# Gate matrix of a product-key expert layer: one-hot rows in 16-bit numbers, the weight in three 8-bit parts, rows made for four tokens at once

## Chip, cores and metric

One Trainium2 chip, one core. The metric is the device time of one execution in microseconds (us); lower is better.

## What is computed

The reference runs two transformer blocks on 256 tokens of width 1024. The change touches one step of the second block, which is done once in each of its two layers: the product-key expert layer (`peer_ffn`).

```python
def peer_ffn(h, w_q, sub_keys, u_tab, v_tab):
    q = (h @ w_q).reshape(B, S, PEER_HEADS, 2, PEER_DQ // 2)
    scores = jnp.einsum('bshpd,hpkd->bshpk', q, sub_keys)
    s1, i1 = lax.top_k(scores[..., 0, :], PEER_TOPK)
    s2, i2 = lax.top_k(scores[..., 1, :], PEER_TOPK)
    # ... the best 16 of the 16x16 pairs: ids = i1 * 128 + i2
    gate = jax.nn.softmax(top_s, axis=-1)
    ...
        u = u_tab[idx]
        act = gelu(jnp.einsum('thkd,td->thk', u, hx))
        return jnp.einsum('thk,thkd->td', g * act, v_tab[idx])
```

There are 128 x 128 experts and 8 heads, and each head chooses 16 experts for each token, so a token has 128 chosen pairs (first key, second key), each with a weight.

## The kernel before

**No gather.** The kernel multiplies with all experts. For each of 128 first keys n it makes the hidden values of 128 experts for 256 tokens (`up(n)` on TensorE, 24 products of 128x256, since each 32-bit product is made of a rounded high part and a low part), takes the gelu into `slots[:, n, :]` (arena), multiplies by the gates, and runs the second product (`down(n)`). Gates of experts that were not chosen are zero.

**The gates.** Those of tokens 128 to 255 go through a table in DRAM that GpSimd scatters into. Those of tokens 0 to 127 are made on chip, and this is what the change is about. For one token, the gate matrix (second key by first key) is a sum over its 128 choices of a one-hot row of the second key, times a one-hot row of the first key, times the weight. With the choices on the partitions this is one TensorE product of 128x128 by 128x128: `second_rows` (one-hot of the second key) is the stationary operand, `first_rows` (one-hot of the first key, times the weight) the moving one. Both are 32-bit numbers, and the trace shows each such product as two matmul records with two weight loads.

**Groups.** Four tokens are a group (`GROUP`), so there are 32 groups (`N_GROUPS`) in each layer. VectorE makes the rows of a group in `gate_rows(j)`: one TENSOR_TENSOR of 128x512 for `second_rows` (L3210) and four TENSOR_SCALAR of 128x128 for `first_rows` (L3214), one for each token because the weight and the key are scalars of the token's column in `keyed`. Both row tensors have two buffers. TensorE runs `gates(j)` (the four products, into a PSUM bank `Y[j % 4]`, "gather" in the trace), then `up(96 + j)`. VectorE then multiplies the known activations by the gates straight from PSUM (`weigh(j)`, L3224), and ScalarE stores the gates of first keys whose activations are not there yet (`late(j)`), which `late_weigh` (L3234) applies later.

**Order of the work.** Every engine's order is written out by hand. TensorE: `up(0)` to `up(95)`, with three transposes near the end that bring the choices and weights of the 128 tokens into `keyed`; then for j = 0 to 31 `gates(j)`, `up(96 + j)`; then the `down` products. VectorE, in the gate stage: `gate_rows(0)`, the low part of a weight tile (`low`, L3089, ring_low, 128x1024), and then for each j `gate_rows(j + 1)`, `weigh(j)`, `late_weigh(j - 1)`, one `low`. A `low` is what TensorE needs for the `up` of its tile, and it is made two tiles ahead. `rows_ready` is counted by VectorE and waited for by `gates(j)`; `gates_filled` is counted by TensorE and waited for by `weigh(j)` and, two groups later, by `gate_rows`; `gates_stored` is counted by ScalarE and waited for by `gates(j + 4)`. The class `Chain` adds a semaphore count to an instruction (`add`) and waits for it on the same engine (`wait`); `chain.wait()` waits for the last one added.

Of the kernel before, what the change touches and what calls it, by code (L numbers as in the profile page):

```python
# [19 lines left out]
BF16 = mybir.dt.bfloat16  # L20
R32 = mybir.dt.float32r
ALU = mybir.AluOpType
# [4 lines left out]
P = 128  # L27
T = 256
# [16 lines left out]
PEER_HEADS, NKEYS, TOPK = 8, 128, 16  # L45
# [22 lines left out]
GROUP = 4  # L68
# [54 lines left out]
     ("cmp_bias", TT * HEADS * N_CMP), ("cmp_valid", TT)])  # L123
CMP_PITCH = 16
BIASES = 3
CMP_COLS = GROUPS * CMP_PITCH
MEM_FIRST = 2
MEM_FILL = {n: (2 * n, 2 * n + 2) if n < 8 else (n + 8, n + 9) for n in range(1, 24)}
# [53 lines left out]
def build(nc, stream, tiles_in, keys_in, ada_in, c_in, xT_in, rows_in, tables_in, final_in, params_in, consts_in, attn_in,  # L182
          masks_in, out):
    ctx = ExitStack()
    with ctx:
# [5 lines left out]
        def S(name):  # L191
            if name not in semaphores:
                semaphores[name] = ctx.enter_context(nc.semaphore(name))
            return semaphores[name]
# [24 lines left out]
        keyed = sb("keyed", [P, 3, T])  # L219
        identity = consts[:, CONSTS["identity"]:CONSTS["identity"] + P]  # L220
        mean_mat = consts[:, CONSTS["mean"]:CONSTS["mean"] + P]
        iota = consts[:, CONSTS["iota"]:CONSTS["iota"] + P]
# [9 lines left out]
        slots = arena[:, :].rearrange("p (i t) -> p i t", t=T)  # L232
# [5 lines left out]
        def carve(at, *shape, memory=arena):  # L238
            n = math.prod(shape)
            view = memory[:, at:at + n]  # L240
            if len(shape) == 2:
                return view.rearrange("p (a b) -> p a b", b=shape[1])
            if len(shape) == 3:
                return view.rearrange("p (a b c) -> p a b c", b=shape[1], c=shape[2])
            assert len(shape) == 1
            return view
# [47 lines left out]
        expert_low = dense.take(4, T)  # L294
        ring_words = ring[:, :, :].rearrange("p s w -> p (s w)")
        rows = Place(gate_rows_at, SLOTS * PIECE, ring_words)
        first_rows = rows.take(2, GROUP, NKEYS)
        second_rows = rows.take(2, GROUP, NKEYS)
        late_act = rows.take(2, P)
        rows.take(P)  # L300
        gates_at = rows.at + P
        weights = rows.take(TT, PEER_HEADS, TOPK)
        offsets = rows.take(PEER_HEADS, TOPK).bitcast(U32)
# [57 lines left out]
        k_mem.append(a.take(2, T))  # L361
        head_bias = a.take(BIASES, P + T)

# [6 lines left out]
        b = Place(ada.at, NKEYS // 2 * T)  # L370
# [23 lines left out]
        Y = [ctx.enter_context(nc.psum_tensor(f"gather{i}", [P, 512], F32)) for i in range(4)]  # L394
# [7 lines left out]
        def mm(out, lhsT, rhs, start, stop):  # L402
            return nc.tensor.matmul(out, lhsT, rhs, start=start, stop=stop, skip_group_check=True)  # L403
# [307 lines left out]
        def bias_of(u):  # L711
            if u["kind"] == "mla":
                return attn_const("future", TT * T)[:, u["tt"] * T:u["tt"] * T + u["w"]]
            return head_bias[:, u["index"] % BIASES, u["tt"] * P:u["tt"] * P + u["w"]]

# [83 lines left out]
        def _(pe):  # L799
# [687 lines left out]
            def peer(l):  # L1487
# [3 lines left out]
                g0 = N_GROUPS * l  # L1491
# [44 lines left out]
                def gates(j, turns=0):  # L1536

                    pe.wait_ge(S("rows_ready"), g0 + j + 1 + 12 * turns)
                    if j >= 4:
                        pe.wait_ge(S("gates_stored"), g0 + j - 3 + 12 * turns)  # L1540
                    for b in range(GROUP):
                        last = mm(Y[j % 4][:, b * NKEYS:(b + 1) * NKEYS], second_rows[:, j % 2, b, :],
                                  first_rows[:, j % 2, b, :], True, True)
                    last.then_inc(S("gates_filled"), 1)

                def down_mm(n, tt, b, high, first=False):
# [776 lines left out]
        def _(dve):  # L2323
            chain = Chain(dve, S("vector_chain"))
            V = nc.vector

            def wide(ap, n):

                return ap.unsqueeze(1).to_broadcast([ap.shape[0], n, ap.shape[1]])
# [786 lines left out]
            def peer(l):  # L3116
# [3 lines left out]
                g0 = N_GROUPS * l  # L3120
# [81 lines left out]
                lows.until(ahead - 1)  # L3202
                dve.wait_ge(S("keyed_ready"), 3 * (l + 1))

                def gate_rows(j):

                    if j >= 2:
                        dve.wait_ge(S("gates_filled"), g0 + j - 1)
                    t = slice(GROUP * j, GROUP * (j + 1))
                    V.tensor_tensor(second_rows[:, j % 2, :, :], wide(iota, GROUP),  # L3210
                                    keyed[:, 1, t].unsqueeze(2).to_broadcast([P, GROUP, NKEYS]), ALU.is_equal)
                    for b in range(GROUP):
                        at = GROUP * j + b
                        last = V.tensor_scalar(first_rows[:, j % 2, b, :], iota, keyed[:, 0, at:at + 1],  # L3214
                                               keyed[:, 2, at:at + 1], ALU.is_equal, ALU.mult)
                    last.then_inc(S("rows_ready"), 1)

                def weigh(j):

# [30 lines left out]
                def down(n, turns=0):  # L3250
# [4 lines left out]
                    if n + 4 < NKEYS:  # L3255
                        hidden_low(n + 4, turns)

                gate_rows(0)
                lows.until(ahead)
                for j in range(N_GROUPS):  # L3260
# [79 lines left out]
        def _(pool):  # L3340
# [62 lines left out]
            for h in range(HEADS):  # L3403
                if h >= BIASES:
                    pool.wait_ge(S("scores_ready"), UNIT_BASE[1] + biased_unit(h - BIASES) + 1)
                slope = -alibi_slopes(HEADS)[h]
                nc.gpsimd.tensor_scalar(head_bias[:, h % BIASES, 0:P], distance[:, 0:P], slope, None, ALU.mult)
                nc.gpsimd.tensor_scalar(head_bias[:, h % BIASES, P:P + T], distance[:, T:2 * T], slope, None, ALU.mult)\
                    .then_inc(S("bias_ready"), 1)
# [239 lines left out]
```

## Time and profile before

| | us |
|---|---|
| median of 3 runs (2925.16 to 2927.48) | 2926.2 |
| the profiled execution, by its own clocking | 2923.19 |
| its span in the trace | 2921.4 |

| engine | busy us | share of the span |
|---|---|---|
| TensorE, matmul | 2895.0 | 99% |
| TensorE, weight load | 2595.1 | 89% |
| VectorE | 2252.5 | 77% |
| ScalarE | 1548.8 | 53% |
| GpSimd | 706.4 | 24% |

The granted clock of TensorE is full in the whole span. TensorE's matmuls overlap one another, so its busy share says that it has work, not how fast it runs: what it costs is the distance from the start of one matmul to the start of the next. The gate stage of the first layer runs from 1543.57 to about 1661.7 us, that of the second from 2445.15 to about 2563.3 us.

### The profile page before, as it was taken

What the parts mean: (1) busy time and instruction counts of PE and PEld (TensorE: products, weight loads), DVE (VectorE), ACT (ScalarE), POOL (GpSimd) and SP (SyncE); (2) the same over time, 40 slices, a digit from 0 to 9 for tenths busy, and PEclk for the clock granted to TensorE, in tenths of its full rate; (3) what the DMA queues carried; (4) which work ended last, traced back from release to release, by engine and by line L of the source; (5) the groups of instructions that cost most, each with busy time, mean ns of one, the idle gap of its engine ahead of it and who ended that gap; (6) DMA issues with size and microseconds to landing.
All of it is one profiled execution on the core that took longest, in us unless ns stands there. A gap on an engine that the chain in (4) does not pass through costs nothing. (4 is left out here: it accounts for less than half of the span.)

```text
span 2921.4 us, 53132 instructions
## 1 busy us (share of the span) xinstructions
PE 2895.0 (99%) x18354; PEld 2595.1 (89%) x18354; DVE 2252.5 (77%) x4303; ACT 1548.8 (53%) x2587; POOL 706.4 (24%) x542
## 2 busy tenths in 40 slices
PE   9999999999999999999999999999999999999998
PEld 8887888888688899899999988888899999988887
DVE  8885888888676789788869866667778887966666
ACT  5546544555654465555554455555655554455444
POOL 0020111101210000027777011110107777311110
PEclk9999999999999999999999999999999999999999
DMA  8773786876256653257776466786357776566775
GB/s 341 285 290 125 256 303 243 324 290 229 84 175 235 210 200 103 95 173 187 188 188 154 162 216 217 235 284 234 132 174 187 188 188 166 150 205 217 217 217 173
DMA packets 201302, 601.61 MB, mean 206 GB/s; under 512 B 53072, under 2 KB 85968, under 8 KB 173904
## 3 DMA queue, kind: packets, MB, share of 16 engines
q1 hardware_dynamic: 142176, 521.19, 52.8%
q0 software_dynamic: 58272, 75.66, 10.9%
q10 hardware_dynamic: 720, 3.00, 0.3%
q8 instruction: 81, 1.33, 0.2%
q14 instruction: 53, 0.43, 0.0%
HBM read 581.81 MB, written 17.96 MB: 205 GB/s over the span
## 5 line engine op out<-in xcount | busy, mean ns | idle before, releaser
L1674 ACT ACTIVATE dense<-ring 128x1024 fp32r<-128x1024 f32 x542 | 573.4, 1058 | 371.8 <-PE gather L403 341.9
L3089 DVE TENSOR_TENSOR ring_low<-ring,dense 128x1024 fp32r<-128x1024 f32 x542 | 660.9, 1220 | 127.1 <-ACT dense L1674 126.1
L403 PE MATMUL turn<-expert_src_high,ring_low 128*128 128x256 f32 x2600 | 725.0, 279 | 0.0
L403 PE MATMUL turn<-expert_src_high,dense 128*128 128x256 f32 x2288 | 645.5, 282 | 0.3
L3426 POOL DMA_INDIRECT gates<-ring x256 | 483.1, 1887 | 664.5 <-DVE ring L3193 409.1
L403 PE MATMUL turn<-expert_src_low,dense 128*128 128x256 f32 x2288 | 636.4, 279 | 0.0
L403 PE MATMUL gather<-dense 128*128 128x512 f32 x2048 | 631.6, 389 | 0.0
L403 PEld LDWEIGHTS turn<-expert_src_high,ring_low 128*128 128x128 f32 x2600 | 488.7, 188 | 0.0
L403 PE MATMUL turn<-rounded 128*128 128x512 f32 x1392 | 480.1, 390 | 0.5 <-DVE rounded L2507 0.5
L403 PEld LDWEIGHTS gather<-dense 128*128 128x128 f32 x2048 | 384.4, 188 | 80.0
L403 PEld LDWEIGHTS turn<-expert_src_high,dense 128*128 128x128 f32 x2288 | 430.3, 188 | 0.7 <-DVE ring_low L3089 0.7
L403 PEld LDWEIGHTS turn<-expert_src_low,dense 128*128 128x128 f32 x2288 | 429.4, 188 | 0.0
L403 PE MATMUL gather<-ring_low,dense 128*128 128x512 f32 x1024 | 398.4, 389 | 0.0
L403 PE MATMUL turn<-rounded,ring_low 128*128 128x256 f32 x1392 | 386.7, 283 | 2.4 <-DVE ring_low L2541 1.2
L2541 DVE TENSOR_TENSOR ring_low<-ring,rounded 128x1024 fp32r<-128x1024 f32 x262 | 325.2, 1247 | 78.2 <-ACT rounded L1674 78.0
L1674 ACT ACTIVATE arena<-turn 128x256 f32<-128x256 f32 (+13 forms) x365 | 154.0, 423 | 344.0 <-PE turn L403 325.3
L1674 ACT ACTIVATE rounded<-ring 128x1024 fp32r<-128x1024 f32 x262 | 274.2, 1053 | 82.7 <-PE gather L403 79.0
L403 PEld LDWEIGHTS turn<-rounded 128*128 128x128 f32 x1392 | 260.8, 188 | 55.0 <-DVE rounded L2507 0.7
L3239 DVE TENSOR_TENSOR dense<-arena,dense 128x256 fp32r<-128x256 f32 x256 | 108.3, 425 | 247.1 <-ACT dense L1674 247.1
L403 PEld LDWEIGHTS turn<-rounded,ring_low 128*128 128x128 f32 x1392 | 260.8, 189 | 5.0 <-issue 1.5
L3416 POOL DMA_DIRECT2D ring<-gates x128 | 91.0, 711 | 664.1 <-DVE arena L3248 634.9
L403 PEld LDWEIGHTS gather<-ring_low,dense 128*128 128x128 f32 x1024 | 192.2, 188 | 39.6
(329 smaller groups left out, 4152.4 us busy)
## 6 DMA issues: line engine op xcount, KB each, us to landing
ring<-tiles_in SPq DMA_DIRECT2D x544, 512.0 KB
ring<-stream SPq DMA_DIRECT2D x204, 1024.0 KB, 5.8
arena<-ada_in POOLq DMA_DIRECT2D x96, 512.0 KB, 5.0
gates<-keyed SPq DMA_DIRECT2D x16, 1024.0 KB, 8.1
ring<-gates POOLq DMA_DIRECT2D x128, 128.0 KB, 3.4
arena<-tables_in POOLq DMA_DIRECT2D x6, 1024.0 KB, 7.6
gates<-ring POOLq DMA_INDIRECT x256
arena<-keys_in SPq DMA_DIRECT2D x2, 1024.0 KB, 7.7
```

Of the source, the lines that this page charges most:

```text
L403: return nc.tensor.matmul(out, lhsT, rhs, start=start, stop=stop, skip_group_check=True)
L1674: return nc.scalar.activation(out, in_, func, **kw)
L2541: V.tensor_tensor(ring_low[:, slot_of(q), cols].bitcast(R32), ring[:, slot_of(q), cols], w_high[:, 2 * (i % 2) + b, :], ALU.subtract).then ...
L3089: V.tensor_tensor(tile_words(t, ring_low).bitcast(R32), tile_words(t), tile_high[:, t % AHEAD, :], ALU.subtract).then_inc(S("tile_low"), 1)
L3239: V.tensor_tensor(expert_low[:, n % 4, :].bitcast(R32), slots[:, n + 12 * turns, :], expert_high[:, n % 4, :], ALU.subtract).then_inc(S("e ...
L3416: pool.dma_start(gate_tiles[:, s, :, :], gates_by_pair[l][n + GATE_SLOTS * turns])\
L3426: pool.indirect_dma_start(gates_flat[l], bass.IndirectOffsetOnAxis(offsets[:, h, c:c + 1], 0), weights[:, 1, h, c:c + 1], None, bounds_che ...
```

## The change

`iota` copied to 16-bit numbers, four times each, becomes `steps`; the two chosen keys become `choice_bits`; the weight is split into three 16-bit numbers of 8 significant bits each, which add up to it (`weight_bits`). This is done once in each layer in `exact_parts()`, ahead of `gate_rows(0)`. In `gate_rows` one comparison makes the second rows of four tokens, one the first rows of four tokens (a single buffer, `first_rows`), and one multiplication makes the three weighted copies `first_parts`. The token is now the innermost index in these tiles, so TensorE reads them at a step of four 16-bit numbers. `gates(j)` has three products for each token, twelve for a group, which add up in PSUM. `gate_rows` gets one more wait, on `rows_ready` of the group before.

```diff
@@ -123,6 +123,7 @@
+PARTS = 3
@@ -294,10 +295,17 @@
         rows = Place(gate_rows_at, SLOTS * PIECE, ring_words)
-        first_rows = rows.take(2, GROUP, NKEYS)
-        second_rows = rows.take(2, GROUP, NKEYS)
+        first_parts = rows.take(2, PARTS * GROUP * NKEYS // 2).bitcast(BF16)\
+            .rearrange("p j (w i b) -> p j w i b", w=PARTS, b=GROUP)
+        second_rows = rows.take(2, GROUP * NKEYS // 2).bitcast(BF16).rearrange("p j (i b) -> p j i b", b=GROUP)
         late_act = rows.take(2, P)
+        steps = carve(rows.at, GROUP * NKEYS // 2, memory=ring_words).bitcast(BF16)\
+            .rearrange("p (i b) -> p i b", b=GROUP)
         rows.take(P)
+        first_rows = keyed[:, 0, 0:GROUP * NKEYS // 2].bitcast(BF16).rearrange("p (i b) -> p i b", b=GROUP)
+        weight_rest = keyed[:, 0, 0:P]
+        weight_bits = keyed[:, 1, 0:PARTS * P // 2].bitcast(BF16).rearrange("p (w t) -> p w t", w=PARTS)
+        choice_bits = slots[:, NKEYS - 2, P:T].bitcast(BF16).rearrange("p (i t) -> p i t", i=2)
@@ -1539,8 +1547,9 @@
                     for b in range(GROUP):
-                        last = mm(Y[j % 4][:, b * NKEYS:(b + 1) * NKEYS], second_rows[:, j % 2, b, :],
-                                  first_rows[:, j % 2, b, :], True, True)
+                        for w in range(PARTS):
+                            last = mm(Y[j % 4][:, b * NKEYS:(b + 1) * NKEYS], second_rows[:, j % 2, :, b],
+                                      first_parts[:, j % 2, w, :, b], w == 0, w == PARTS - 1)
                     last.then_inc(S("gates_filled"), 1)
@@ -3202,18 +3211,39 @@
+                def exact_parts():
+
+                    V.tensor_copy(steps, iota.unsqueeze(2).to_broadcast([P, NKEYS, GROUP]))
+                    for i in range(2):
+                        chain.add(V.tensor_copy(choice_bits[:, i, :], keyed[:, i, 0:P]))
+                    chain.wait()
+                    chain.add(V.tensor_copy(weight_bits[:, 0, :], keyed[:, 2, 0:P]))
+                    chain.wait()
+                    chain.add(V.tensor_tensor(weight_rest, keyed[:, 2, 0:P], weight_bits[:, 0, :], ALU.subtract))
+                    chain.wait()
+                    chain.add(V.tensor_copy(weight_bits[:, 1, :], weight_rest))
+                    chain.wait()
+                    chain.add(V.tensor_tensor(weight_bits[:, 2, :], weight_rest, weight_bits[:, 1, :], ALU.subtract))
+                    chain.wait()
+
                 def gate_rows(j):
                     if j >= 2:
                         dve.wait_ge(S("gates_filled"), g0 + j - 1)
+                    if j >= 1:
+                        dve.wait_ge(S("rows_ready"), g0 + j)
                     t = slice(GROUP * j, GROUP * (j + 1))
-                    V.tensor_tensor(second_rows[:, j % 2, :, :], wide(iota, GROUP),
-                                    keyed[:, 1, t].unsqueeze(2).to_broadcast([P, GROUP, NKEYS]), ALU.is_equal)
-                    for b in range(GROUP):
-                        at = GROUP * j + b
-                        last = V.tensor_scalar(first_rows[:, j % 2, b, :], iota, keyed[:, 0, at:at + 1],
-                                               keyed[:, 2, at:at + 1], ALU.is_equal, ALU.mult)
-                    last.then_inc(S("rows_ready"), 1)
+
+                    def of(i):
+                        return choice_bits[:, i, t].unsqueeze(1).to_broadcast([P, NKEYS, GROUP])
+
+                    chain.add(V.tensor_tensor(first_rows, steps, of(0), ALU.is_equal))
+                    V.tensor_tensor(second_rows[:, j % 2, :, :], steps, of(1), ALU.is_equal)
+                    chain.wait()
+                    V.tensor_tensor(first_parts[:, j % 2, :, :, :],
+                                    first_rows.unsqueeze(1).to_broadcast([P, PARTS, NKEYS, GROUP]),
+                                    weight_bits[:, :, t].unsqueeze(2).to_broadcast([P, PARTS, NKEYS, GROUP]),
+                                    ALU.mult).then_inc(S("rows_ready"), 1)
@@ -3255,6 +3285,7 @@
+                exact_parts()
                 gate_rows(0)
                 lows.until(ahead)
```

## Rows read from the trace of the kernel before

**Rows 1.** The page, busy time of each engine over the span.
```profile
PE 2895.0 (99%) x18354; PEld 2595.1 (89%) x18354; DVE 2252.5 (77%) x4303; ACT 1548.8 (53%) x2587; POOL 706.4 (24%) x542
```
**Rows 2.** Windows: length, busy us and instructions of each engine, clock; gate stages 1, 2.
```profile
core 0: us, PE busy (x) PEld busy (x) DVE busy (x) ACT busy (x) POOL busy (x), PEclk, DMA share, GB/s
1543.57:1661.70 118.13, 118.13 (x1022) 118.13 (x1021) 111.38 (x253) 52.88 (x131) 46.59 (x32) 1.00 0.54 148
2445.17:2563.30 118.13, 118.13 (x1023) 118.13 (x1022) 111.38 (x253) 52.87 (x131) 54.39 (x36) 1.00 0.54 148
```
**Rows 3.** Timeline of TensorE, gate products of both layers: start, us, operation, count.
```profile
1543.57 1.05 PE L403 MATMUL gather<-ring 128*128 128x128 f32 x8
...
1658.46 1.05 PE L403 MATMUL gather<-ring 128*128 128x128 f32 x8
...
2445.15 1.05 PE L403 MATMUL gather<-ring 128*128 128x128 f32 x8
```
**Rows 4.** Timeline of VectorE ahead of the gate stage of layer 1.
```profile
1505.60 1.23 DVE L3089 TENSOR_TENSOR ring_low<-ring,dense 128x1024 fp32r<-128x1024 f32 x1 [1.57 <-ACT dense L1674]
1508.40 1.23 DVE L3089 TENSOR_TENSOR ring_low<-ring,dense 128x1024 fp32r<-128x1024 f32 x1 [1.57 <-ACT dense L1674]
...
1539.20 1.23 DVE L3089 TENSOR_TENSOR ring_low<-ring,dense 128x1024 fp32r<-128x1024 f32 x1 [1.58 <-ACT dense L1674]
1540.34 0.68 DVE L3210 TENSOR_TENSOR ring<-consts,keyed 128x512 f32<-128x512 f32 x1
1540.95 1.11 DVE L3214 TENSOR_SCALAR ring<-consts,keyed 128x128 f32<-128x128 f32 x4
```
**Rows 5.** Timeline of VectorE, one group near the end of the stage.
```profile
1652.39 0.67 DVE L3224 TENSOR_TENSOR arena<-arena,gather 128x500 f32<-128x500 f32 x1
1652.98 0.27 DVE L3234 TENSOR_TENSOR arena<-arena,ring 128x116 f32<-128x116 f32 x1
1653.17 1.22 DVE L3089 TENSOR_TENSOR ring_low<-ring,dense 128x1024 fp32r<-128x1024 f32 x1
1654.30 0.68 DVE L3210 TENSOR_TENSOR ring<-consts,keyed 128x512 f32<-128x512 f32 x1
1654.90 1.11 DVE L3214 TENSOR_SCALAR ring<-consts,keyed 128x128 f32<-128x128 f32 x4
1655.93 0.68 DVE L3224 TENSOR_TENSOR arena<-arena,gather 128x504 f32<-128x504 f32 x1
```
**Rows 6.** Waits inside the gate stage of layer 1: who for whom, us, times, longest.
```profile
DVE arena L3224 <- PE gather L403: 5.9, 21, 1.3
```
**Rows 7.** Groups of TensorE instructions by form: busy us, mean ns.
```profile
L403 PE MATMUL turn<-expert_src_high,ring_low 128*128 128x256 f32 x2600 | 725.0, 279 | 0.0
L403 PE MATMUL gather<-dense 128*128 128x512 f32 x2048 | 631.6, 389 | 0.0
L403 PE MATMUL gather<-ring 128*128 128x128 f32 x512 | 67.4, 275 | 0.0
L403 PE MATMUL gather<-ring,arena 128*128 128x64 f32 x8 | 1.1, 278 | 0.0
L403 PE MATMUL gather<-arena,ring 128*128 128x30 f32 x4 | 0.5, 253 | 0.0
L403 PEld LDWEIGHTS turn<-expert_src_high,ring_low 128*128 128x128 f32 x2600 | 488.7, 188 | 0.0
```
**Rows 8.** Weight loads of transposes (one line's instructions): duration ns min/median/max.
```profile
L820 PEld LDWEIGHTS gather<-consts,arena x126: 138/141/143, 191.4 to 2122.9; 128*128 128x128 f32 x126
```
**Rows 9.** Timeline of TensorE at products with few moving columns.
```profile
516.29 0.53 PE L403 MATMUL gather<-arena,ring 128*128 128x30 f32 x4
...
516.63 0.97 PEld L403 LDWEIGHTS gather<-ring,arena 128*128 128x128 f32 x8
516.66 1.08 PE L403 MATMUL gather<-ring,arena 128*128 128x64 f32 x8
```
**Rows 10.** Groups of VectorE instructions: count, busy us, mean ns, idle before.
```profile
L3089 DVE TENSOR_TENSOR ring_low<-ring,dense 128x1024 fp32r<-128x1024 f32 x542 | 660.9, 1220 | 127.1 <-ACT dense L1674 126.1
L3248 DVE TENSOR_TENSOR arena<-arena,ring 128x256 f32 (+1 forms) x128 | 53.6, 419 | 0.0
L3210 DVE TENSOR_TENSOR ring<-consts,keyed 128x512 f32<-128x512 f32 x64 | 43.8, 684 | 0.0
L2552 DVE CAST rounded<-hidden 128x256 fp32r<-128x256 f32 x88 | 25.9, 295 | 3.0
L2389 DVE TENSOR_SCALAR arena<-arena,keyed 128x512 f32<-128x512 f32 x20 | 10.0, 543 | 0.4
L3138 DVE CAST ring<-ring 128x64 f32<-128x64 uint32 x16 | 4.0, 247 | 0.0
```
**Rows 11.** Timeline of VectorE, instructions that wait for the one before.
```profile
1491.33 0.18 DVE L3187 TENSOR_REDUCE ring<-ring 128x2 f32<-128x32 f32 x1
1491.54 0.17 DVE L3190 RECIPROCAL ring<-ring 128x2 f32<-128x2 f32 x1
```

## The prediction, made before the changed kernel was built or run

> **What bounds the kernel now.** I read the page first: TensorE is busy 99% of the span, VectorE 77% [rows 1]. The change acts only in two stretches, so I looked at the windows over them: in each gate stage of 118.13 us TensorE has no idle time, and VectorE is busy 111.38 us, 94% [rows 2]. So TensorE sets the pace and VectorE is close behind; any theory must price both. ScalarE, at 53 of 118 us, is no candidate. The first gate products of layer 1 start at 1543.57 and the last at 1658.46, 31 groups later: a group takes 3.706 us [rows 3]. Ahead of the stage, where TensorE runs `up` alone, VectorE's low parts step from 1505.60 to 1508.40, held by the tiles, so an `up` takes 2.80 us [rows 4]. The four gate products of a group therefore cost 3.706 - 2.80 = 0.906 us, which is 0.113 us for each of the eight records. VectorE's demand is 111.38 / 32 = 3.48 us a group. It waits for the gate products before `weigh` only 5.9 us in a stage [rows 6]: it catches up with TensorE and then waits a little.
>
> **TensorE, part by part.** Removed: eight records at 0.113, 0.906 us a group. Added: twelve 16-bit products of 128 moving columns, each with its load of 128 stationary columns. No row shows a 16-bit product, so I bound one. *Lower bound, the stream alone:* a record of 512 columns lasts 389 ns, of 256 columns 279 ns [rows 7]; 256 columns are 110 ns, 128 columns 55 ns, and twelve make 0.66 us. *Upper bound, the load alone:* the eight records with only 64 moving columns last 1.08 us in all; taking one record of 0.278 us off and dividing by seven, their starts are 0.115 us apart [rows 7, 9], no less than with 128 columns. There the 32-bit weight load sets the step. If a 16-bit load is no faster, twelve make 12 x 0.115 = 1.38 us. *Value taken:* a load is not always that long. It lasts 188 ns in an ordinary product [rows 7] but 141 ns in a transpose [rows 8], 47 ns less for the same 128 columns. A 16-bit load moves half the bytes, so I put it next to the quick one: 0.111 - 0.047 = 0.064 us a product (0.111 is the step of the eight gate records, (1.05 - 0.275) / 7 [rows 3, 7]). Twelve make 0.77 us. A group saves 0.906 - 0.77 = 0.136 us, and 64 groups 8.7 us. The repeated stationary operand I count as loaded each time: an `up` uses one high part twice in a row and the trace still has one load for each record [rows 1].
>
> A rule speaks against this value. The Trainium skill (TensorE: Matmul & The Clock Gate, section Back-to-back issue gap) says that in a real stream of weight load and matmul pairs with 128 moving columns the spacing is about 81 ns. No run here shows it yet; by it the twelve would take 0.97 us, and the change would cost some 4 us of TensorE time in place of saving 9.
>
> **VectorE, the rows of a group.** Removed: the stretch from the comparison's start at 1654.30 to the next instruction's at 1655.93, 1.63 us (0.60 for L3210, 1.03 for the four L3214) [rows 5]. Added: two comparisons of 512 and one multiplication of 1536 elements in 16 bits. No row has 16-bit operands. Two-tensor rows go by elements: 256 in 419 ns, 512 in 684, 1024 in 1220 [rows 10], 1.04 ns an element. *Upper bound,* the same per element: 684, 684 and 1220 + 512 x 1.047 = 1756 ns. *Lower bound,* by bytes: 512 short numbers are 256 words, 419 ns; 1536 are 768 words, halfway between 684 and 1220, 952 ns. One-tensor rows show that the engine can go at twice the pace: a scalar operation on 512 takes 543 ns against 684 [rows 10], and the four at 128 start 0.26 us apart, (1.11 - 0.34) / 3 [rows 5]. I take the lower bound, because the new tiles have four tokens side by side, so every operand is read in whole runs of words. The starts of following instructions lie about 0.08 us before the end of the last [rows 5], so the three take 0.34 + 0.34 + 0.87 = 1.55 us, 0.08 less than now. The wait between them costs nothing: the first comparison ends while the second runs. The added wait on `rows_ready` is on a multiplication one whole group back, with `weigh` and a low part between; behind it in VectorE's queue stand the rows of the next group, `weigh` and the low part, but it is over when it is reached. VectorE's demand becomes 3.48 - 0.08 = 3.40 us a group, under TensorE's 2.80 + 0.77 = 3.57. The rows are made one group ahead of their use, so they stay hidden.
>
> The Trainium skill (VectorE: DVE Perf Modes, section The perf-mode tier table) gives a two-tensor operation on 16-bit SBUF data two elements a cycle and one on 32-bit data one. The second half agrees with the 1.04 ns above; of the first no run here shows anything yet.
>
> **The start of the stage.** `exact_parts` stands ahead of `gate_rows(0)`, on a path that has little slack: the rows are begun at 1540.34 and end at 1542.06 [rows 4], and TensorE asks for them at 1543.57 [rows 3], 1.5 us later. By start-to-start steps: the copy of 512 (543 ns, the scalar row) 0.46; two casts of 128, between 247 ns for 64 and 295 for 256, say 0.26, less the overlap, so 0.18 and, as it is waited for, 0.29; two waited-for casts of the weight at 0.29; two subtractions of 128, about 0.29 by the 1.04 ns slope under the 419 ns row, 0.32 with the wait. The gap behind a waited-for instruction is 0.03 us: 1491.33 + 0.18 to 1491.54 [rows 11]. The sum is 0.46 + 0.18 + 0.29 + 2 x 0.29 + 2 x 0.32 = 2.15 us. Rows(0) then end at 1540.34 + 2.15 + 0.34 + 0.34 + 0.95 = 1544.12, and TensorE stalls 0.55 us, with the signal 0.6. Behind it in VectorE's queue are the low part for tile 97 and `gate_rows(1)`, both wanted a group later, so they lose nothing. Without the 1.5 us of slack the whole 2.1 us would show. Layer 2 has the same sequence [rows 2, 3]. TensorE stays the bound afterwards, so 2 x 0.6 = 1.2 us remain.
>
> **Sum.** -8.7 + 1.2 = -7.5 us. Against the profiled execution's own 2923.2 (span 2921.4 and 1.8 around it) that is 2915.7; the median of the runs is 3.0 higher, so the forecast is 2926.2 - 7.5 = 2918.7 us. Its own range, with a product between 0.058 and 0.072 us and a stall of 0.3 to 1.5 us, is 2914 to 2925.
>
> **Rivals.** A measurement of this kernel can tell about 0.2%, 5.9 us, from no change.
>
> 1. *The weight load stays at its 32-bit pace (slower).* On TensorE, in `gates(j)`: twelve products at 0.115 are 1.38 us, 0.474 more than now; 64 times and the 1.2 make +31.5, 2957.7 us. It decides from a step of 0.0755 us, where twelve cost what eight cost now. For it: four more loads a group, in a stage in which loads and streams are equally long. Against: the quick load [rows 8]. The step of 0.081 of the rule above lies between, and so does the 0.092 of the four records with 30 columns, (0.53 - 0.253) / 3 [rows 7, 9]: at the mean of 0.064 and 0.115, 0.09, the group costs 1.08 us, 2938.5 us; at 0.08, 0.96 us, 2930.9 us.
> 2. *VectorE at one element a clock (slower).* The rows take 0.60 + 0.60 + 1.68 = 2.88 us, the demand is 3.48 + 1.25 = 4.73 us against 3.70, VectorE becomes the bound and TensorE waits for `rows_ready`: 32 x 1.02 = 33 us a layer, less about 2.6 us of rows made ahead, 2 x 30 = +60, 2986 us. For it: no two-tensor row is faster. Against: the halved bytes.
> 3. *Streams alone count (faster).* If products that share a stationary operand are not held by its reload, TensorE needs 2.80 + 0.66 = 3.46 us, VectorE 3.40, about even; 64 x 0.246 - 1.2 is -14.5, and some of it is lost to VectorE's late, long groups: 2914 us at most.
>
> **How the numbers follow.** Forecast 0.42, rival 3 0.10, a step between 0.075 and 0.10 0.18, rival 1 in full 0.14, rival 2 0.16. The range reaches from the streams alone, 2911.5, to the full load, 2958, and leaves out rival 2. Faster by over 0.2%: most of the forecast's case and rival 3, 0.45. Within 0.2%: the forecast's slow edge and the low end of the steps between, 0.14. Slower: 0.41.
>
> **What would show it.** Starts of gate groups 3.57 us apart in place of 3.706; twelve records with starts 0.064 apart; comparisons at 420 ns and the multiplication at 950; VectorE still waiting for gates before `weigh`; one TensorE gap near 0.6 us ahead of the first group of each layer. If the comparisons last 680 ns, the prediction fails by rival 2; if the twelve take over 0.9 us, by rival 1.

## The result and the profile after

The changed kernel is slower: 2958.14 us (median of four runs, 2957.95 to 2961.07) against 2926.84 us (2925.16 to 2928.52) for the kernel before, measured beside it. The ratio on record is 1.0115, with a 95% interval of 1.0103 to 1.0126 (the two medians alone give 1.0107). The prediction was 2918.7 us with a range up to 2958.0, so the measured time lies 0.14 us outside the range, on the side opposite to the forecast. It is within half a us of the time worked out for rival 1, 2957.7 us; the runs below show that the mechanism of this rival was another one.

The page of the changed kernel, busy time of each engine (beside [rows 1]):

```profile
span 2956.3 us, 53590 instructions
PE 2929.4 (99%) x18610; PEld 2625.1 (89%) x18610; DVE 2250.0 (76%) x4189; ACT 1549.2 (52%) x2587; POOL 715.0 (24%) x542
```

TensorE is still the engine that always has work, VectorE even has slightly less. The span is 34.9 us longer than that of the kernel before (2956.3 against 2921.4). The windows over the first gate stage from its second to its last group, 30 groups (beside [rows 2]):

```profile
core 0: us, PE busy (x) PEld busy (x) DVE busy (x) ACT busy (x) POOL busy (x), PEclk, DMA share, GB/s
1548.37:1675.47 127.10, 127.10 (x1082) 125.28 (x1081) 103.45 (x182) 48.65 (x120) 44.80 (x28) 1.00 0.47 128
```

The clock is full, TensorE has no idle time, VectorE is busy 81% of the stretch where it was 94%. The time is inside TensorE's own queue. Timeline of TensorE, start and us (beside [rows 3]):

```profile
1544.15 1.57 PE L411 MATMUL gather<-ring 128*128 128x128 bf16 x12 [0.28 <-DVE ring L3243]
1545.48 0.36 PE L411 MATMUL turn<-expert_src_high,dense 128*128 128x256 f32 x1
...
1548.37 1.58 PE L411 MATMUL gather<-ring 128*128 128x128 bf16 x12
1549.71 0.36 PE L411 MATMUL turn<-expert_src_high,dense 128*128 128x256 f32 x1
...
1675.47 1.59 PE L411 MATMUL gather<-ring 128*128 128x128 bf16 x12
```

From 1544.15 to 1675.47 are 31 groups, so a group takes 4.236 us where it took 3.706. The twelve gate products hold the queue from 1548.37 to 1549.71, 1.34 us, 0.112 us for each. The difference, 0.530 us, times 64 groups is 33.9 us, and a stall at the start of each stage brings it to the 34.9 us of the span. The same reading of the kernel before:

```profile
1562.09 1.05 PE L403 MATMUL gather<-ring 128*128 128x128 f32 x8
1562.90 0.37 PE L403 MATMUL turn<-expert_src_high,dense 128*128 128x256 f32 x1
1563.10 0.28 PE L403 MATMUL turn<-expert_src_low,dense 128*128 128x256 f32 x1
1563.22 0.28 PE L403 MATMUL turn<-expert_src_high,ring_low 128*128 128x256 f32 x1
```

Its eight records hold the queue for 0.81 us, and the `up` behind them takes the other 2.90 us of the group, before and after alike: its second product starts 0.20 us behind its first, where the next ones follow 0.12 us apart. So the gate products went from 0.81 to 1.34 us, and the `up` did not move. What kind of time the gate products' is, the groups by form tell (busy us, mean ns; stretch of the first stage; beside [rows 7]):

```profile
L411 PE MATMUL gather<-ring 128*128 128x128 bf16 x377 | 49.9, 297 | 0.3 <-DVE ring L3243 0.3
L411 PEld LDWEIGHTS gather<-ring 128*128 128x128 bf16 x378 | 40.2, 118 | 2.3 <-DVE ring L3243 0.5
```

Here lies the surprise. The weight load is short, 118 ns against 188: the 16-bit load is quicker, as the forecast had it. But the matmul record lasts 297 ns. By [rows 7] a record of 256 columns at one a clock lasts 279 ns and one of 512 lasts 389, so 128 columns should make 224. These 128 columns take as long to stream as some 300 would. One thing about them is new: TensorE reads them at a step of four numbers.

### The profile page after: what moved, and what is told of

The parts are those of the page before. It is cut to its first block and busy times, and to the rows that moved or that the text cites. A ratio compares the mean times of both kernels' runs of the same rounds, so it can differ in the third digit from the quotient of the medians.

```text
span 2956.3 us, 53590 instructions
## 1 busy us (share of the span) xinstructions
PE 2929.4 (99%) x18610; PEld 2625.1 (89%) x18610; DVE 2250.0 (76%) x4189; ACT 1549.2 (52%) x2587; POOL 715.0 (24%) x542
## 5 line engine op out<-in xcount | busy, mean ns | idle before, releaser
L3457 POOL DMA_INDIRECT gates<-ring x256 | 491.5, 1920 | 660.6 <-DVE ring L3202 409.3
```

Source lines behind the costliest of these rows:

```text
L3457: pool.indirect_dma_start(gates_flat[l], bass.IndirectOffsetOnAxis(offsets[:, h, c:c + 1], 0), weights[:, 1, h, c:c + 1], None, bounds_che ...
```

## The experiments

Three theories could give 0.112 us a product. *Stream*: the moving operand at a step of four streams at half pace. *Step of the load*: the loaded operand at a step of four loads slowly. *Load as such*: 128 columns take 0.11 us to load whatever their size. In the runs that read other numbers than they should, VectorE's work, every instruction and every size stay as they are, so only TensorE's addresses differ.

### Which operand it is

The edits, in `gates(j)`:

```diff
 # e1: moving operand adjacent; e2: loaded operand adjacent; e3: both
-    mm(Y..., second_rows[:, j % 2, :, b], first_parts[:, j % 2, w, :, b], ...)
+    # e2, e3: second_rows[:, j % 2, :, :].rearrange("p i b -> p (i b)")[:, b * NKEYS:(b + 1) * NKEYS]
+    # e1, e3: first_parts[:, j % 2, w, :, :].rearrange("p i b -> p (i b)")[:, b * NKEYS:(b + 1) * NKEYS]
```

> The changed kernel, but TensorE reads each moving operand of a gate product from 128 adjacent 16-bit numbers in place of every fourth one; the numbers are then the wrong ones, so the gates of tokens 0 to 127 are not computed rightly, while every instruction and its size stay. The loaded operand keeps its step of four. Theory 'stream' (the moving operand read at a step of four streams at half pace; a gate record lasts 297 ns where 168 + 53 = 221 was to be expected): records fall to about 220 ns, twelve products from 1.34 to about 0.77 us, the group from 4.24 to about 3.6 us, the kernel by 64 x 0.6 = 38 us to about 2920. Theory 'step of the load' and theory 'load as such' (a 128-column load takes 0.11 us each time): no change, 2958.

> The changed kernel, but the loaded (stationary) operand of a gate product is read from 128 adjacent 16-bit numbers in place of every fourth; the gates of tokens 0 to 127 are not computed rightly, every instruction and its size stay. The moving operand keeps its step of four. Theory 'step of the load': twelve products fall from 1.34 to about 0.77 us, the kernel to about 2920. Theory 'stream' and theory 'load as such': no change, 2958 within 3 us.

> The changed kernel with both operands of the gate products read from 128 adjacent 16-bit numbers; the gates of tokens 0 to 127 are not computed rightly, every instruction and its size stay. Theory 'load as such': still 0.11 us for a product, 2958. Theory 'stream': the same as with the moving operand alone packed, about 2920. If both steps matter and each alone hides the other, only this one falls to about 2920 and the two before it stay at 2958.

Moving operand adjacent: 2917.8 us. Loaded operand adjacent: 2956.0 us. Both: 2916.5 us (nine runs, 2914.95 to 2919.51; ratio to the kernel before 0.9973, 0.9963 to 0.9983). The first two are single runs. With the moving operand adjacent, groups of TensorE's gate products by form, and the timeline; then the groups with the loaded one adjacent, and the load with both adjacent:

```profile
L411 PE MATMUL gather<-ring 128*128 128x128 bf16 x372 | 26.7, 221 | 0.3 <-DVE ring L3244 0.3
L411 PEld LDWEIGHTS gather<-ring 128*128 128x128 bf16 x372 | 21.9, 115 | 1.8 <-DVE ring L3244 0.5
```

```profile
1547.02 0.86 PE L411 MATMUL gather<-ring 128*128 128x128 bf16 x12 [0.29 <-DVE ring L3244]
1547.69 0.36 PE L411 MATMUL turn<-expert_src_high,dense 128*128 128x256 f32 x1
...
1657.39 0.86 PE L411 MATMUL gather<-ring 128*128 128x128 bf16 x12
```

```profile
L411 PE MATMUL gather<-ring 128*128 128x128 bf16 x324 | 41.9, 293 | 0.3 <-DVE ring L3244 0.3
L411 PEld LDWEIGHTS gather<-ring 128*128 128x128 bf16 x324 | 34.1, 113 | 1.6 <-DVE ring L3244 0.5
```

```profile
L411 PEld LDWEIGHTS gather<-ring 128*128 128x128 bf16 x303 | 17.0, 98 | 1.1
```

With the moving operand adjacent its record falls to 221 ns, twelve products to 1547.69 - 1547.02 = 0.67 us, the group to (1657.39 - 1547.02) / 31 = 3.560 us. With the loaded one adjacent little changes. The theory 'stream' holds; the other two fall. The load's step of four costs little. Packing it alone takes the group from 4.236 to 4.200 us (starts from 1544.23 to 1674.43 in e2), 2.3 us in 64 groups, which is the difference between the two kernels. Packing it on top of the other shortens its record from 115 to 98 ns, but the group takes 3.566 us (1543.94 to 1654.49 in e3) against 3.560, so nothing is gained. The 1.3 us between the kernel times of e1 and e3 arise ahead of the first gate stage, as told below the table of steps.

### What each product costs

The changed kernel without the third product of each token; the lowest part of the weight is made but left out of the sum.

```diff
-                        for w in range(PARTS):
+                        for w in range(2):
                             ...
-                                      first_parts[:, j % 2, w, :, b], w == 0, w == PARTS - 1)
+                                      first_parts[:, j % 2, w, :, b], w == 0, w == 2 - 1)
```

> The changed kernel without the third of the three products for each token (the lowest part of the weight is made but left out of the sum): 8 products for a group in place of 12. By every theory in which a product costs its own 0.1115 us (1.34 / 12), a group falls by 0.446 us to 3.79 and the kernel by 28.5 us to 2929.5, some 3 us above the kernel before, where eight records of 32-bit numbers cost 0.81 to 0.91 us. If a fixed cost of changing between 16-bit and 32-bit products were most of it, the gain would be well below 28 us.

Measured: 2929.24 us (ratio 1.0016, 1.0006 to 1.0026). Four products of 64 groups less are 28.9 us less, 0.113 us each; in the traces the group falls from 4.236 to 3.766 us ((1660.49 - 1543.74) / 31), 0.118 us each. So the time is the products' own, and no fixed cost of changing between 16-bit and 32-bit products is most of it. It also says that at this pace even two parts would have gained nothing.

### How the pace depends on the step

The moving operand at other steps, from the same tile:

```diff
+    flat = first_parts[:, j % 2, :, :, :].rearrange("p w i b -> p (w i b)")
+    # step s = 3, 8 (step 2 likewise within one part): flat[:, at:at + s * (NKEYS - 1) + 1:s]
```

> The changed kernel, but the moving operand of each gate product is every second 16-bit number in place of every fourth (from the same tile, so the gates of tokens 0 to 127 are not computed rightly); all else stays. Before this, adjacent numbers gave 0.056 us a product and a step of four 0.1115. Theory 'only adjacent numbers stream at full pace': still 0.11 us, 2958. Theory 'distance in bytes' (four bytes are what a 32-bit operand steps by, and those stream at full pace): 0.056 us a product, the group 3.57 us, 2917. Something between, 0.08, would mean a cost that grows with the distance, 2935.

> The changed kernel, but the moving operand of each gate product is every third 16-bit number (6 bytes apart) in place of every fourth; the gates of tokens 0 to 127 are not computed rightly, all else stays. Step 1 and step 2 gave 0.056 and 0.059 us a product, step 4 gave 0.1115. If the pace falls in one step at a distance of 8 bytes, this gives 0.06 us and about 2920; if the cost grows evenly with the distance from step 2 on, 0.085 us and about 2938; if everything over 4 bytes is at half pace, 0.11 us and 2957.

> The changed kernel with the moving operand of each gate product at every eighth 16-bit number (16 bytes apart); the gates of tokens 0 to 127 are not computed rightly, all else stays. If the pace is full up to some distance and half beyond it, as at step 4: 0.11 us a product and 2957. If the cost grows with the distance: 0.2 us or more a product, 12 x 0.1 x 64 = 77 us more, 3030 or more.

Timeline of TensorE, the twelve gate products and the first `up` behind them, at step 2, 3 and 8, one fence for each:

```profile
1563.23 0.90 PE L411 MATMUL gather<-ring 128*128 128x128 bf16 x12
1563.94 0.37 PE L411 MATMUL turn<-expert_src_high,dense 128*128 128x256 f32 x1
```

```profile
1555.73 1.26 PE L411 MATMUL gather<-ring 128*128 128x128 bf16 x12
1556.77 0.37 PE L411 MATMUL turn<-expert_src_high,dense 128*128 128x256 f32 x1
```

```profile
1559.33 2.94 PE L411 MATMUL gather<-ring 128*128 128x128 bf16 x12
1561.90 0.48 PE L411 MATMUL turn<-expert_src_high,dense 128*128 128x256 f32 x1
```

| step of the moving operand, 16-bit numbers | bytes spanned by 128 columns | twelve products, us | one, us | group, us | kernel, us |
|---|---|---|---|---|---|
| 1 (e1, one run) | 256 | 0.67 | 0.056 | 3.560 | 2917.8 |
| 2 (e5, one run) | 512 | 0.71 | 0.059 | 3.605 | 2922.5 |
| 3 (e6, one run) | 768 | 1.04 | 0.087 | 3.95 | 2943.0 |
| 4 (changed kernel) | 1024 | 1.34 | 0.112 | 4.236 | 2958.1 |
| 8 (e7, one run) | 2048 | 2.57 | 0.214 | 6.03 | 3077.8 |

The times of the gate products and of the group (mean over the first stage) are safer here than those of the kernel. In the traces of e1, e5, e6, e7 and e9, and in that of f1 below, the granted clock was 0.50 for 10 to 14 us in all, in two or three stretches near 276, 520 and 800 us, and the first gate stage began at 1547.0 to 1548.8 us; in the other traces that was 0 to 3.4 us, and the stage began at 1543.2 to 1544.4. These 3 to 5 us lie ahead of anything that the runs change.

From step 2 on a product costs 0.027 to 0.030 us for each unit of the step. In bytes, the stream goes over the row at 2048 / 0.214 = 9.6 bytes a ns at a step of eight, 9.1 at four, 8.8 at three and 8.7 at two, gaps included. Adjacent numbers take 56 ns, near one column a clock, 128 / 2.4 = 53 ns at the full clock of 2.4 GHz. Of the expectations for e5, 'distance in bytes' came nearest (0.059 us a product against 0.056), of those for e6 the even growth came true (2943.0 against 2938), and so did that of e7.

The time of e7 holds one thing more. 64 x (2.57 - 1.34) = 79 us would make 3037. The clock is most of the rest. Windows and timeline of e7:

```profile
1550.00:1640.00 90.00, 90.00 (x535) 71.74 (x534) 50.63 (x90) 23.43 (x59) 41.30 (x28) 0.91 0.39 89
1563.00:1566.00 3.00, 3.00 (x16) 3.00 (x16) 2.68 (x5) 0.24 (x1) 2.39 (x3) 0.50 0.17 0
```

```profile
1562.46 0.28 PE L411 MATMUL turn<-expert_src_high,dense 128*128 128x256 f32 x1
...
1563.10 0.41 PE L411 MATMUL turn<-expert_src_low,dense 128*128 128x256 f32 x1
1563.31 0.41 PE L411 MATMUL turn<-expert_src_high,ring_low 128*128 128x256 f32 x1
...
1566.22 0.28 PE L411 MATMUL turn<-expert_src_low,dense 128*128 128x256 f32 x1
```

The granted clock is 0.91 on average, and 0.50, the 1.2 GHz level, behind the twelve slow streams that began at 1559.33: there the `up` products step by 0.21 us in place of 0.12, and that `up` takes 4.56 us. Over the two stages the clock is at 0.50 for some 65 us in all, which at half pace costs about 32 us. Another 0.1 us a group, 6 us, is the last slow stream reaching into the `up`, which takes 3.00 us at the least behind it in place of 2.90, and 4 us lie ahead of the stage. With the 79 that is 121 us, where the kernel grew by 120. In the changed kernel, with streams half as slow, the clock in the stages stayed at 1.00, and so it did in e9 below, where eight streams as slow as these run in each group.

### Is it a matter of 16 bits?

The kernel before, with its 32-bit moving operand at a step of two and of four:

```diff
-                                  first_rows[:, j % 2, b, :], True, True)
+    flat = first_rows[:, j % 2, :, :].rearrange("p b i -> p (b i)")
+    # e8: flat[:, b // 2 * 2 * NKEYS + b % 2:][every 2nd]; e9: flat[:, b:b + 4 * NKEYS - 3:4]
```

> The kernel before (32-bit rows, four products for a group, two records each), but the moving operand is every second 32-bit number, so 8 bytes apart; the gates of tokens 0 to 127 are not computed rightly, all else stays. If it is the distance in bytes that counts, 8 bytes are at half pace here too: each record goes from 107 to 213 ns of stream, a group from 0.9 to some 1.75 us, the kernel by 54 us to about 2978. If the half pace belongs to 16-bit numbers that are not side by side, nothing changes, 2925.

> The kernel before (32-bit rows, four products for a group), but the moving operand is every fourth 32-bit number, 16 bytes apart; the gates of tokens 0 to 127 are not computed rightly, all else stays. The rule that fits the runs so far: a stream of 128 columns takes the longer of its own cycles and of the bytes it spans at 9.6 bytes a ns (step 4 of 16-bit numbers: 1024 bytes, 0.107 us; step 8: 2048 bytes, 0.213). A 32-bit record of 128 columns lasts 107 ns of stream anyway, so 8 bytes apart cost nothing. With 16 bytes apart it spans 2048 bytes: 0.213 us for each of eight records, the group 0.85 us longer, the kernel by 54 us to about 2979. If 32-bit streams are not slowed by distance at all: 2924.

Measured, one run each: 2923.6 us at step 2, beside 2924.95 for the kernel before, and 2986.3 us at step 4, beside 2923.15. The expectation for e8 gave two outcomes and the second came true. That does not mean what it said there, that words are exempt: e9 shows them slowed. The groups by form of e8 and of e9:

```profile
L403 PE MATMUL gather<-ring 128*128 128x128 f32 x193 | 26.0, 275 | 0.0
```

```profile
L403 PE MATMUL gather<-ring 128*128 128x128 f32 x153 | 38.0, 403 | 0.0
```

32-bit gate records start 0.111 us apart at a step of one already, and in that time about 1024 bytes can be passed over, which is just a step of two; e8's groups take 3.713 us against 3.706. Whether those 0.111 us are the stream itself or the 32-bit load is not told apart: the record lasts as long as an `up` record of 256 columns, 275 and 279 ns, but one of 64 columns lasts 278 too [rows 7]. At a step of four it spans 2048 bytes, and the record lasts 403 ns, close to the 409 of a 16-bit one that spans as much. It grows by 128 ns where the rule at 9.6 bytes a ns says 107; the kernel grew by 63 us where 54 were expected, of which 4 to 5 lie ahead of the stage. So the rule holds within some 20% for words too: what counts is the distance in bytes, not the format, and a step that costs nothing behind a slower 32-bit product can take twice the time of a quick 16-bit one.

### Full kernels that avoid the step

Two kernels have all of the computation. In *f4* the first rows are made for two tokens side by side, so TensorE reads at a step of two (4 bytes); the order of the parts is changed so that VectorE's three instructions stay three. In *f1* the weight's parts go into the second rows, which are loaded, and the plain one-hot first rows are made token by token and streamed.

```diff
 # f4
+    first_parts: "p j (h w i b) -> p j h w i b", h=2, w=PARTS, b=2
+    last = mm(Y..., second_rows[:, j % 2, :, b], first_parts[:, j % 2, b // 2, w, :, b % 2], ...)
 # f1
+    V.tensor_tensor(first_rows[:, j % 2, :, :], wide(iota, GROUP), choice_bits[:, 0, t].unsqueeze(2)..., ALU.is_equal)
+    last = mm(Y..., second_parts[:, j % 2, w, :, b], first_rows[:, j % 2, b, :], ...)
```

> A full kernel, all of it computed: the changed kernel with the first rows made for two tokens side by side in place of four, so that TensorE reads the moving operand at a step of two; the rows of the four tokens still come from one comparison and one multiplication, whose token operands are now read two adjacent numbers at a time. Theory 'distance in bytes' for TensorE: 0.67 us for the twelve products, group 3.57, 2917 to 2920. Theory 'only adjacent numbers': 2958. For VectorE: if runs of two 16-bit numbers are read as fast as runs of four, comparison 0.42 and multiplication 0.95 us; if not, up to 0.68 and 1.75, with which VectorE needs some 4.3 us a group and the kernel takes 2960 or more.

> A full kernel, all of it computed: the weight's three parts go into the second rows, which TensorE loads (step of four, which cost nothing so far), and the plain one-hot first rows are the moving operand, made with each token's 128 numbers adjacent. TensorE then needs 0.67 us for twelve, 3.47 to 3.57 us a group. But the comparison of the first rows reads one number of a token again and again, and VectorE does it at one element a clock, 0.68 us in place of 0.42: its demand rises from 3.40 to 3.66 us a group and becomes the bound. Expected 2926 within 4 us, no gain or loss against the kernel before. If VectorE did it in 0.42 us, 2917.

f4: 2919.97 us, ratio 0.9984 (0.9975 to 0.9994). VectorE's comparison took 0.42 us and its multiplication 0.95, so a run of two numbers is read as fast as one of four. Its group takes 3.605 us, as in e5. f1: 2923.02 us, ratio 0.9995 (0.9985 to 1.0005), no difference. VectorE's groups and the window in f1, and the two places where TensorE idled around the end of the first stage:

```profile
L3242 DVE TENSOR_TENSOR ring<-keyed 128x1536 bf16<-128x1536 bf16 x27 | 25.7, 952 | 0.0
L3239 DVE TENSOR_TENSOR ring<-consts,arena 128x512 bf16<-128x512 f32 x27 | 18.5, 685 | 0.0
L3237 DVE TENSOR_TENSOR keyed<-ring,arena 128x512 bf16<-128x512 bf16 x27 | 11.3, 419 | 0.0
```

```profile
1550.00:1640.00 90.00, 90.00 (x910) 88.91 (x910) 90.00 (x151) 40.68 (x100) 76.08 (x26) 1.00 0.60 147
```

```profile
1654.80 0.86 PE L411 MATMUL gather<-ring 128*128 128x128 bf16 x12 [0.32 <-DVE ring L3242]
...
1663.12 0.47 PE L411 MATMUL gather<-dense 128*128 128x512 f32 x1 [0.89 <-DVE dense L3268]
```

Its first-row comparison takes 685 ns, in which one operand is 32-bit and the other repeats one number; which of the two costs it the pace was not told apart. VectorE is busy 90.00 of 90.00 us, so it has no slack left. But it is not yet what sets TensorE's pace in this window: TensorE has no idle time either, and its 910 records are as many as in the same window of e3. VectorE's backlog shows only at the end, as 0.32 and 0.89 us of idle TensorE. The time came out as expected (2926 within 4); that VectorE is the bound throughout did not.

The last one, *f5*, is f4 with a 16-bit format of 11 significant bits, so that two parts carry 22 bits of the weight in place of 24, and a token needs two products.

```diff
-BF16 = mybir.dt.bfloat16
-PARTS = 3
+BF16 = mybir.dt.float16
+PARTS = 2
+        rows.take(GROUP * NKEYS)      # keeps what lies behind the rows in its place
```

> All of the computation is there: as f4_pairs, but with two parts of 11 significant bits (16-bit floating point with a longer fraction) in place of three of 8, so two products for a token and a multiplication of 1024 elements in place of 1536. If a step of two streams at full pace and this format goes like the other: TensorE 8 x 0.056 = 0.45 us, group 2.90 + 0.45 = 3.35, VectorE's demand 3.40 - 0.27 = 3.13; 64 x 0.36 - 1 = 22 us gained on the kernel before, 2903. If the step of two streams at half pace: 8 x 0.11 = 0.89, 2928.

Measured: 2903.06 us (four runs, 2901.08 to 2904.56), ratio 0.9927 (0.9911 to 0.9944), 20.6 us faster than the kernel before. Timeline of TensorE and the groups of f5:

```profile
1543.21 0.66 PE L413 MATMUL gather<-ring 128*128 128x128 f16 x8
...
1647.55 0.66 PE L413 MATMUL gather<-ring 128*128 128x128 f16 x8
```

```profile
L413 PE MATMUL gather<-ring 128*128 128x128 f16 x224 | 18.6, 224 | 0.0
L3250 DVE TENSOR_TENSOR ring<-keyed 128x1024 f16<-128x1024 f16 x29 | 19.8, 684 | 0.0
```

A group takes (1647.55 - 1543.21) / 31 = 3.366 us. It is the fastest kernel of this study.

## Why the prediction was wrong, point by point

**What bounds the kernel.** Right. TensorE sets the pace before and after, with no idle time in the stage.

**TensorE: the value taken, 0.064 us a product.** This is the step that failed. It measured 0.112 us, twelve made 1.34 us in place of 0.77, and 64 times the 0.57 us between them is 36 us. The reasoning on the load was right: it took 118 ns, even shorter than the 141 taken as its neighbour. What was missing is the other operand. The lower bound priced the stream by its columns, from rows of operands whose numbers are adjacent, and nowhere was a price put on the step of four that the change introduces, though the diff shows it. With only this removed (e1) the kernel took 2917.8 us; the sum had said 2918.7. That these two agree is in part luck, since two terms of the sum miss in opposite directions and cancel there: adjacent products cost 0.056 us in place of 0.064, 0.1 us less for twelve, and the next term was 0.1 us too large.

**What is removed: 0.906 us.** This term was mis-sized too. It was the group less an `up` of 2.80 us, taken from a stretch in which `up` runs alone [rows 4]. Behind gate products an `up` takes 2.90 us, in the kernel before and in the changed one, and the eight records held the queue for 0.81 us. The sum took away 0.1 us a group more than was there, 6 us in all. On the profiled executions the forecast was 2915.7 us and the measured time 2958.13, 42 us apart: 36 from the products and 6 from this term. (The medians are only 39 us apart because the forecast put the median 3 us above the profiled execution, and in the changed kernel the two are the same.)

**The rule against this value.** The Trainium skill's spacing of about 81 ns (TensorE: Matmul & The Clock Gate, section Back-to-back issue gap) did not show either: adjacent numbers gave 56 ns, a step of four 112. The Trainium skill (TensorE: Matmul & The Clock Gate, section Weight-path perf modes) says that 16-bit weights of 128 columns load in a fast mode, packed or strided. The load records agree so far that at either step they are well under the 188 ns of 32 bits: 98 ns where both operands are adjacent, 113 to 118 in the other runs. On steps, the Trainium skill (SBUF — State Buffer, the note on cachelines) says that two hits in each line of 16 bytes are needed for full bandwidth, and puts the stride that is free at up to eight 16-bit or four 32-bit numbers. For a moving operand it is not so here: a step of four 16-bit numbers, two hits a line, is at half pace, one of three at two thirds, one of eight at a quarter, and a 32-bit record at a step of four lasted 403 ns in place of 275.

**Rival 1.** Its time came out, 2957.7 us against 2958.1, and its mechanism was wrong. It held the load to its 32-bit pace; e1 and the load records show a quick load. That the time agrees so closely is luck: it put the twelve at 1.38 us and what they replace at 0.906, 0.474 more a group, where 1.34 and 0.81 were measured, 0.53 more, and the 3 us between median and profiled execution filled what was missing. The chance of 0.14 was given to the load alone; the cause that led to this time had none.

**VectorE, the rows.** Right. Timeline of VectorE in the changed kernel, start of the first stage (beside [rows 4, 5]):

```profile
1540.49 0.42 DVE L3216 CAST ring<-consts 128x512 bf16<-128x512 f32 x1
1540.82 0.36 DVE L3218 CAST arena<-keyed 128x128 bf16<-128x128 f32 x2
1541.22 0.31 DVE L3220 CAST keyed<-keyed 128x128 bf16<-128x128 f32 x1
...
1542.47 0.42 DVE L3240 TENSOR_TENSOR keyed<-ring,arena 128x512 bf16<-128x512 bf16 x1
1542.81 0.42 DVE L3241 TENSOR_TENSOR ring<-ring,arena 128x512 bf16<-128x512 bf16 x1
1543.15 0.95 DVE L3243 TENSOR_TENSOR ring<-keyed 128x1536 bf16<-128x1536 bf16 x1
1544.02 1.21 DVE L3098 TENSOR_TENSOR ring_low<-ring,dense 128x1024 fp32r<-128x1024 f32 x1
```

0.42, 0.42 and 0.95 us, from start to start 0.34 + 0.34 + 0.87 = 1.55, each as worked out. Rival 2 had no part in it. The Trainium skill's two elements a cycle for a two-tensor operation on 16-bit data (VectorE: DVE Perf Modes, section The perf-mode tier table) agrees: 512 elements took 0.42 us and 1536 took 0.95, 0.52 ns for each element more, half of the 1.04 ns of 32-bit numbers. VectorE's demand was 103.45 / 30 = 3.45 us a group, where 3.40 had been said.

**The start of the stage.** Right. `exact_parts` took 1542.47 - 1540.49 = 1.98 us for 2.15, and the first gate products began at 1544.15. Before, they began at 1543.57; the stage is 0.15 us later in this run (1540.49 against 1540.34), so 0.43 us are left for the stall, where 0.55 to 0.6 was said; the row shows 0.28 us of idle matmul before it.

**Rival 3.** Half right. A product with adjacent numbers costs 0.056 us, the stream alone, where the forecast's case had 0.064. Twelve made 0.67, within 0.01 of the bound. The gain of e3 was still only 8 us in place of 14, and the 0.1 us a group by which the `up` behind them is longer than 2.80 accounts for 6 of these. VectorE was busy nearly all the time in e1, as the rival had it, but no row shows TensorE held by it inside the stage, and in the changed kernel, where VectorE is busy only 81%, the `up` takes the same 2.90 us. Window of e1:

```profile
1550.59:1657.39 106.80, 106.80 (x1083) 105.54 (x1081) 104.09 (x183) 48.63 (x120) 50.54 (x28) 1.00 0.53 152
```

**The range.** It ended at the full load, 2958, and was missed by 0.14 us. A bound made of one mechanism's exact price, with the whole of that case meant to lie inside, left no room for the spread of the runs (2957.95 to 2961.07).

## What to carry to other kernels

When a layout is changed to suit one engine, price how the other one reads it: here the token was made innermost so that VectorE reads whole runs, and TensorE's moving operand paid for it. Put the operand that must be read at a step on the loading side (f1, which gained nothing here because its rows cost VectorE more), or keep the step of the moving side within four bytes (pairs of 16-bit numbers), which served both engines. When a bound of an unmeasured operation is taken from rows, check that these rows read their operands the way the new operation will. And take the cost of a block that is removed from its own rows (here from its first start to the start of what follows it, 0.81 us) rather than as a difference to another stretch of the kernel (0.906).

## What the runs showed of the hardware

- A moving operand of 128 columns streams at the slower of one column a clock (53 ns at the full clock) and about 9 bytes of span a ns: 0.056, 0.059, 0.087, 0.112 and 0.214 us a product at steps of 1, 2, 3, 4 and 8 16-bit numbers (8.7 to 9.6 bytes a ns). Other numbers of columns were not run.
- A loaded 16-bit operand of 128 columns costs little more at a step of four than adjacent: 0.036 us in a group of twelve beside a moving operand at a step of four, nothing beside an adjacent one. Its record lasts 113 to 118 ns, 98 where both operands are adjacent, and a 32-bit one 188.
- The matmul record shows the step: it lasts 221 ns with adjacent numbers, 297 at a step of four and 409 at eight. Whoever goes by its length alone would read it as one of more columns.
- The stages with very slow streams (step 8) also lost the full clock at times: 0.91 granted on average in 1550 to 1640 us, with stretches at 0.50 in which `up` products step by 0.21 us in place of 0.12.
